# Who builds the second one-hots of the spread: two each on ScalarE and VectorE, or all four on ScalarE

## The reference, cut to what matters

```python
def peer_ffn(xn, wq, subkeys, u, v):                       # 1152 tokens, 8 heads, 128 x 128 experts, top 16
    q  = (tb @ wq).reshape(PEER_BLOCK, PEER_HEADS, 2, PEER_HALF)
    sc = einsum('thpd,pnd->thpn', q, subkeys)
    sv, si = top_k(sc, 16)                                 # 16 best of each half
    cand   = sv[:, :, 0, :, None] + sv[:, :, 1, None, :]
    cv, ci = top_k(cand, 16)                               # 16 best pairs
    i1, i2 = first half's key, second half's key           # expert e = 128 * i1 + i2
    g = softmax(cv)
    h = einsum('thkd,td->thk', u[e], tb)
    a = gelu(h) * g
    out = einsum('thk,thkd->td', a, v[e])
```

## Time and profile before

| | us |
|---|---|
| median of 3 runs | 3543.74 |
| lowest and highest run | 3539.31, 3547.16 |
| the profiled execution, its own time | 3539.31 |
| its span in the profile | 3537.6 |
| TensorE busy in the span | 3300.8 (93%) |
| VectorE busy | 2640.3 (75%) |
| ScalarE busy | 800.3 (23%) |
| the builds, first and last in the span | 1304.1 to 1650.3 |

### The profile page before, as it was taken

One profiled execution on the slowest core, in us unless ns is written; L12 is line 12 of the kernel. 1 busy time (PEld: TensorE's weight loads), 2 busy tenths in 40 slices (PEclk: granted clock), 3 DMA queues, 4 the chain that ended last, 5 costly groups with the idle time before them and its releaser, 6 DMA issues.

```text
span 3537.6 us, 43678 instructions
## 1 busy us (share of the span) xinstructions
PE 3300.8 (93%) x14507; PEld 1960.5 (55%) x14516; DVE 2640.3 (75%) x5015; ACT 800.3 (23%) x1589; POOL 1494.4 (42%) x1116
## 2 busy tenths in 40 slices
PE   9769999986888899999899999999999999999997
PEld 7436789984465667677544444444444444444443
DVE  2555888845468767775699998888888777888888
ACT  3542112215122337675100001000010000100001
POOL 0000388710223778886234443444443433434342
PEclk9989999988999999999899999999999999999998
DMA  8988699956887679889899999999999999999997
GB/s 351 414 340 302 225 406 401 403 180 214 335 303 262 176 193 200 209 165 202 324 416 395 416 382 417 411 404 405 417 389 415 375 391 401 383 406 399 397 416 285
DMA packets 465464, 1196.04 MB, mean 338 GB/s; under 512 B 195672, under 2 KB 257800, under 8 KB 386568
## 3 DMA queue, kind: packets, MB, share of 16 engines
q0 software_dynamic: 149776, 679.68, 50.2%
q1 hardware_dynamic: 183472, 495.29, 37.0%
q10 hardware_dynamic: 132048, 19.01, 3.6%
HBM read 1124.51 MB, written 70.39 MB: 338 GB/s over the span
## 4 chain that ended last, share of the span: by engine, by line
PE 33%; DVE 11%; DMA 3%; issue 3%; POOL 0%; DVEq 0%; ACT 0%; POOLq 0%
PE k_ps L2689 17%; PE k_ps L2675 16%; DVE k_yacc L2439 5%; DVE d_ring L2425 4%; DMA d_ring<-peer_uv,d_idx 3%; DVE k_acc L2439 0%; DMA out_y<-k_acc 0%; DVE d_a L2447 0%; DVE d_qacc L2457 0%; POOL d_ring L2387 0%; DVE e_topi L2477 0%; DVE d_aw L2434 0%; DVE e_top L2472 0%; DVE e_sc L2474 0%; DVE e_ci L2477 0%
## 5 line engine op out<-in xcount | busy, mean ns | idle before, releaser
L2387 POOL DMA_INDIRECT d_ring<-peer_uv,d_idx x512 | 691.1, 1350 | 1004.8 <-DVEq L2441 900.3
L2675 PE MATMUL k_ps<-k_xd,k_ring 128*128 128x512 f32 x2016 | 889.4, 594 | 7.8 <-DMA k_ring<-u_blocks 5.2
L2675 PEld LDWEIGHTS k_ps<-k_xd,k_ring 128*128 128x128 f32 x2016 | 384.2, 191 | 493.1 <-issue 486.3
L2425 DVE SCALAR_TENSOR_TENSOR d_ring<-d_ring,k_xn 128x1024 f32<-128x1024 f32 x512 | 607.5, 1221 | 53.8 <-DMA d_ring<-peer_uv,d_idx 31.4
L1687 POOL DMA_INDIRECT G<-c_cellg,c_cell x256 | 434.3, 1696 | 114.7 <-issue 88.7
L2689 PE MATMUL k_ps<-k_ring,d_a 128*128 128x512 f32 x1024 | 453.0, 595 | 10.8 <-DVE d_a L2447 10.0
L2689 PE MATMUL k_ps<-d_v,d_a 128*128 128x512 f32 x1024 | 451.6, 594 | 2.4 <-DVE d_qacc L2457 2.2
L2439 DVE SCALAR_TENSOR_TENSOR k_acc<-d_ring,d_aw,k_acc 128x1024 f32<-128x1024 f32 x256 | 328.9, 1285 | 45.8 <-DVE k_acc L2439 29.7
L2439 DVE SCALAR_TENSOR_TENSOR k_yacc<-d_ring,d_aw,k_yacc 128x1024 f32<-128x1024 f32 x256 | 328.9, 1285 | 37.0 <-DVE k_yacc L2439 25.4
L2689 PEld LDWEIGHTS k_ps<-k_ring,d_a 128*128 128x128 f32 x1024 | 195.1, 191 | 259.1 <-issue 257.0
L2634 ACT ACTIVATE d_a<-k_ps 128x512 f32<-128x512 f32 x128 | 76.3, 597 | 1140.5 <-PE k_ps L2675 1108.9
(11 more groups left out here) (423 smaller groups left out, 4265.5 us busy)
## 6 DMA issues: line engine op xcount, KB each, us to landing
c_chunk<-wq SPq DMA_DIRECT2D x128, 512.0 KB
k_ring<-u_blocks SPq DMA_DIRECT2D x128, 512.0 KB, 21.1
s_kc<-sb_kT SPq DMA_DIRECT2D x32, 1024.0 KB, 13.7
s_vc<-sb_v SPq DMA_DIRECT2D x32, 1024.0 KB, 11.2
c_chunk<-w_m SPq DMA_DIRECT2D x64, 512.0 KB
k_ring<-v_blocks SPq DMA_DIRECT2D x64, 512.0 KB, 9.5
d_gb<-G SPq DMA_DIRECT2D x32, 1024.0 KB
d_v<-v_blocks SPq DMA_DIRECT2D x64, 512.0 KB
```

Of the source, the lines that this page charges most:

```text
L2387: pool.indirect_dma_start(out=ring[:, b], out_offset=None, in_=a["peer_uv"], in_offset=bass.IndirectOffsetOnAxis(ap=idx8[par][:, b:b + 1], ...
L2425: last = nc.vector.scalar_tensor_tensor(ring[:, b, 0:D], ring[:, b, 0:D], 1.0, xn[T % 2][:], ALU.mult, ALU.mult, accum_out=h[:, bass.ds(co ...
L2675: last = nc.tensor.matmul(ps[:, HB + x % 2, :], ub[j][:, k], xd[:, k].rearrange("p t q -> p (t q)"), start=(k == 0), stop=(k == KC - 1))
```

## The change

VectorE no longer builds any of `second`; ScalarE builds all four tokens of each quad, in the same two passes. The semaphore `seconds_dve` and TensorE's wait for it go.

```diff
@@ one_hots, VectorE
                         nc.vector.tensor_tensor(first[c % DEEP], ..., ALU.is_equal).then_inc(firsts, 1)
-                        for k in range(QUAD // 2, QUAD):
-                            last = nc.vector.tensor_scalar(second[c % DEEP][:, k], iota[:], turned[:, q, 1, tok + k:tok + k + 1], turned[:, q, 2, tok + k:tok + k + 1], ALU.is_equal, ALU.mult)
-                        last.then_inc(seconds_dve, 1)
@@ second_hots, ScalarE
-                        for k in range(QUAD // 2):
+                        for k in range(QUAD):
                             last = nc.scalar.activation(second[c % DEEP][:, k], iota[:], ACT.Abs, scale=-1.0, bias=turned[:, q, 1, tok + k:tok + k + 1])
                         last.then_inc(distances, 1)
                         act.wait_ge(distances, c + 1)
-                        for k in range(QUAD // 2):
+                        for k in range(QUAD):
                             last = nc.scalar.activation(second[c % DEEP][:, k], second[c % DEEP][:, k], ACT.Relu,
                                                         scale=turned[:, q, 3, tok + k:tok + k + 1], bias=turned[:, q, 2, tok + k:tok + k + 1])
                         last.then_inc(seconds, 1)
@@ spread_out, TensorE
                         pe.wait_ge(firsts, c + 1)
                         pe.wait_ge(seconds, c + 1)
-                        pe.wait_ge(seconds_dve, c + 1)
```

More of the change, by code:

```diff
@@ L1465, in decide @@
         pe_turned, turned_done = sem("c_pe_turned"), sem("c_turned_done")
-        firsts, distances, seconds, seconds_dve = sem("c_firsts"), sem("c_distances"), sem("c_seconds"), sem("c_seconds_dve")
+        firsts, distances, seconds = sem("c_firsts"), sem("c_distances"), sem("c_seconds")
         spread_done, taken = sem("c_spread_done"), sem("c_taken")
```

## The result

The changed kernel takes 3585.68 us (median of 4 runs, 3581.17 to 3591.14) against 3545.45 us for the one before (median of 4, 3539.31 to 3552.22). The ratio is 1.0121, 95% interval 1.0097 to 1.0146: it is slower by 34 to 52 us. The forecast was a median of 3578, range 3560 to 3602. The sum, +34.2 us, was made for the profiled executions; their spans are 3537.6 and 3573.0, which is +35.4. The medians are 40.2 us apart, 6.0 more than the sum, and the changed kernel's lies 7.7 us above the forecast of 3578.

What follows compares the result with a forecast made beforehand. TensorE reaches the barrier before the last phase last, so its delay arrives whole at the end. Queries 29.8 plus pairs 4.4 gave +34.2 us: 3573.5 against the profiled execution, a median of 3578, range 3560 to 3602.

Steps and rivals of the forecast that it cites:

- The sum, +34.2 us: Whole span: 29.8 us from the queries plus 4.4 from the pairs, added to the profiled 3539.3 us.
- What bounds the kernel: Phase before the last: TensorE reaches its closing barrier last, so any delay arrives whole at the end; last phase unchanged.
- The price of a quad: ScalarE's builds: two more Abs and two more Relu cost 1.36 us more a quad, bounds 1.32 to 1.47.
- The queries: Stages 6 to 8: ScalarE's round of 3.69 us replaces TensorE's 2.68; +11.6, +10.9, +7.3, together 29.8 us.
- The pairs: Attention pairs, stages 6 to 8: ScalarE's and VectorE's lists both near their limit; +2.5, +0.3, +1.6, together 4.4 us.
- the walk: Attention pairs, gone through step by step on ScalarE and VectorE; +2.5, +0.3, +1.6 us in stages 6, 7, 8.
- The quads that cost nothing: 11 quads ahead of the queries or beside the merge: hidden by ScalarE's waits; 15 us if the covers were gone.
- the round of 2 x 2.68 us: Queries, rival: TensorE's clock falls to 1.2 GHz, rounds of 5.36 us, 55 and 32 us more, up to 3665; chance 0.08.
- Nothing hides: All 64 quads, rival: each costs its full 1.36 us, 87 us in all, 3631; chance 0.06.
- VectorE paces the pairs: Pairs, rival: VectorE's relief gains 12 us; 3532 if queries stay with TensorE, chance 0.02; 3562 if they cost 30, chance 0.09.

Runs made afterwards that it cites:

- Experiment 1: Kernel before, with only the 33 quads of the queries built wholly on ScalarE, all others split two and two; ratio to before 1.0104.
- 4: Kernel before, with ScalarE building three of four tokens in the queries and VectorE one, elsewhere two and two; ratio to before 0.9987.
- 8: Changed kernel, with the queries' 45 quads copied out of PSUM by VectorE instead of ScalarE; ratio to the kernel before 0.9993.
- the two kernels with 32 fillers: Kernel before and changed kernel, each with 32 tiny memsets added to VectorE's list at the start of the attention phase; ratios to before 0.9968 and 1.0081.
- experiments 2: Kernel before, with only the 20 quads beside the pairs built wholly on ScalarE, all others split two and two; ratio to before 0.9971.
- the changed kernel with fillers: Changed kernel with 32 tiny memsets added to VectorE's list at the start of the attention phase; ratio to the kernel before 1.0081.
- the control: Changed source with every quad split two and two, the same instructions as the kernel before; ratio to before 0.9995.
- experiment 3: Kernel before, with only the 11 quads ahead of the queries and behind the stage built wholly on ScalarE; ratio to before 0.9955.
- 6: Kernel before, with VectorE's part of the second one-hots left out and ScalarE still building its two tokens; ratio to before 0.9985.

## Why the prediction was right, step by step

- **What bounds the kernel.** Right: what the phase loses arrives at the end. The last phase was taken as unchanged; it was 2.3 us shorter, within the 1809.9 to 1812.4 of its kind. That was luck: had the change removed 20 to 40 instructions of VectorE and not 128, some 12 us would have come off that no step of the prediction has.
- **The price of a quad.** Right: 2.81 to 2.87 us a build in the queries of stage 6, where 1.47 + 1.36 = 2.83 was forecast.
- **The queries.** Right in mechanism and size: forecast 11.6, 10.9, 7.3, measured 11.5, 10.8, 7.5. Experiment 1 has it alone, 4 shows the threshold, and 8 that it is ScalarE's list with the takes in it, and neither the builds' own length nor the clock. Wrong in a detail: I had the products 3.7 us apart for 12, 12 and 9 quads, and that TensorE can't run ahead of ScalarE. It keeps rounds of 2.68 us up to the fifth product and waits from then on; the end of the stretch is set by ScalarE's takes either way. The builders' wait is also for the product of six quads back, as the ring has six slots, and not five as I wrote; no term of the sum uses it.
- **The pairs.** The mechanism was right. The size was low, 4.4 against 7.5 between these two profiles; but between the two kernels with 32 fillers, which differ by the same change, it is 2.7 (3.9, -1.5 and 0.3). Only stage 6 repeats: 3.8 to 4.3 us in each of the four kernels that build all beside its pairs on ScalarE, against 2.5 in the walk. For stage 6, the start of L1755 moves by 2.6 us as in the walk (24.5 us from the second to the last before, 28.2 now, with a start 1.1 earlier):

```profile
1309.55 1.21 DVE L1755 SCALAR_TENSOR_TENSOR k_ring<-k_ps,k_ring 128x1024 f32<-128x1024 f32 x1
...
1337.71 1.22 DVE L1755 SCALAR_TENSOR_TENSOR k_ring<-k_ps,k_ring 128x1024 f32<-128x1024 f32 x1 [1.41 <-ACT k_ring L1986]
```

  What was missing stands behind it in TensorE's timeline:

```profile
1320.84 3.78 PE L2134 MATMUL k_ps<-c_soft,c_negtri 128*128 128x512 f32 x4 [3.31 <-DVE c_soft L1755]
1324.41 2.84 PE L2138 MATMUL k_ps<-c_past,c_negone 128*128 128x512 f32 x4
...
1338.99 2.83 PE L2134 MATMUL k_ps<-k_ring,c_negtri 128*128 128x512 f32 x4 [2.03 <-DVE k_ring L1755]
1341.61 2.77 PE L2138 MATMUL k_ps<-c_past,c_negone 128*128 128x512 f32 x4
```

  The same work takes 1.98 and 1.88 us at full clock (as between these rows, at 1331 and 1333). The clock is at its lower level for part of it, twice, behind idle time of 3.31 and 2.03 us: 0.50 from 1320 to 1325 and 0.66 on average from 1340 to 1345, where the kernel before has 1.00 in both windows. The second time lies behind the last L1755, on the path, and costs 1344.22 - 1338.99 = 5.23 us instead of 3.54: the 1.7 us by which stage 6 exceeds the walk. I had such falls in the forecast's range and not in the sum.

  In the other three kernels with these pairs (experiments 2 and 8, and the changed kernel with fillers) the slow piece stands one pair earlier, 3.5 to 3.7 us behind 2.1 us of idle time. Nothing is slow behind the last L1755 there, but it starts 4.0 us later than before instead of 2.6, and the stretch comes to the same 68.3 or 68.4. In the kernels with other splits TensorE waits at most 1.4 us at these last two places, and is at full clock. So the slow piece goes with the lengthened idle time in all four; that the idle time brought it on was not tried alone, and earlier in the stage the clock falls in the control and not in the kernel before, with the same instructions.

  In stage 7 the last L1755 is where the walk had it (39.3 us from the first, 39.2 before), and the remaining 1 us is behind it, at a longer slow stretch too; in the changed kernel with fillers that work is at full clock, and stage 7 is 1.5 us shorter than with two and two. In stage 8 the difference of 2.1 is little more than what the control shows without any change (+1.6).
- **The quads that cost nothing.** Right, by experiment 3 and by the waits that remained.
- **The rivals.** The clock stayed at 1.00 through the queries, so that the round of 2 x 2.68 us never came. The Trainium skill, "TensorE: Matmul & The Clock Gate", section "A second HAM failure mode: psum-queue depth-cycling", tells of another kernel in which the clock went back and forth with short idle times between groups of matmuls. This trace does not show it: waits of 0.7 to 1.9 us in each of the slow rounds left the granted clock at 1.00 in the queries of all three stages. "Nothing hides" fell with experiments 2 and 3, "VectorE paces the pairs" with 6: its relief is worth 4 to 6 us of 12, and only while ScalarE's list is left alone.

## What to carry to other kernels

Before work is moved to an engine that looks idle over the whole span, compare its list with the pace of the stage where the work lands, in start to start times: here the first 0.35 us of a round were free, the first token cost 8 us in all and the second 22. If an engine's list holds both work that can be done ahead (builds) and work that others wait for at once (takes), it is the second kind that carries the delay to them; it may be cheaper to move that. And when a change alters the number of instructions of an engine ahead of a loop, look at the loop's own idle times before the difference is put down to the change.

## What the runs showed of the hardware that was not expected

The number of VectorE instructions ahead of its last loops moves this kernel by 0.3%. At the head of the second and later turns of one or two of these loops VectorE has an idle time of some 10.8 us or some 6 us, three or five times in an execution. How long they are, and in which loops, goes with that number: three long ones with 0, 64 more and 128 fewer, three short ones with 20 to 40 and 83 fewer, five short ones with 32 more and 96 fewer, and both kinds with 66 fewer. Kernels 128 instructions apart behave alike; those 64 apart do not. The last phase is 1810 to 1812 us with three long ones, 1797 to 1800 with three short, 1801 to 1804 with five short, and 1818 with both kinds, in the order of TensorE's own idle time behind them.

The Trainium skill, "Runtime: NRT & Kernel Launch", section "Instruction fetch mechanics", says that a taken branch to a target outside the two pages of instructions that an engine holds waits for a fetch of the target's page. That fits an idle time at the jump back that no semaphore explains. The page gives blocks of 256 instructions, and why kernels 128 apart agree is not explained by that. No run shows the fetch itself, so the cause stays open and only the dependence on the number of instructions is shown.
